# Second block of a two-block model on one core: spatial values and all heads' values projected with tokens in the partitions

## What is computed

```python
h = _rmsnorm(x, norm_w)
(q_raw, ffwd_raw, fbwd_raw, i_raw, ga_raw,
 u_raw, v_raw, gb_raw, ma_raw, mb_raw) = split(einsum('bsd,de->bse', h, w_in))     # ten pieces of 1024
y_a = _hgrn2_branch(q_raw, ffwd_raw, fbwd_raw, i_raw, ga_raw, ...)   # 8 heads of 128, values are i_raw
# the spatial branch:
u = gelu(u_raw)
v = _layernorm(gelu(v_raw), ln_w, ln_b)                              # over the 1024 channels of a token
mixed = einsum('gts,bnsgc->bntgc', w_s, v in chunks of 128 tokens and groups of 128 channels) + b_s
y_b = u * mixed * silu(g_raw)
merged = sigmoid(ma_raw) * (y_a @ w_proj_a) + sigmoid(mb_raw) * (y_b @ w_proj_b)
x = x + merged @ w_out
```

## Time and profile before

| | us |
|---|---|
| median of 3 runs (1718.98 to 1719.69) | 1719.18 |
| the profiled execution | 1719.48 |
| its span in the trace | 1717.7 |
| TensorE busy in it, matmuls | 1703.1 (99%) |
| TensorE busy in it, loads of weights | 1397.5 (81%) |
| VectorE busy | 1149.0 (67%) |
| ScalarE busy | 815.9 (48%) |
| POOL busy | 30.4 (2%) |
| granted clock of TensorE, mean | 0.999 |

### The profile page before, as it was taken

The page is one execution under the profiler, slowest core; times in us unless marked ns, Lnnn a source line. Parts: engine busy times, 40 slices in busy tenths (PEclk is TensorE's granted clock), DMA queues, the critical chain, the costliest instruction groups (busy, mean ns, idle before and its releaser), DMA issues.

```text
span 1717.7 us, 22160 instructions
## 1 busy us (share of the span) xinstructions
PE 1703.1 (99%) x8782; PEld 1397.5 (81%) x8782; DVE 1149.0 (67%) x1686; ACT 815.9 (48%) x1164; POOL 30.4 (2%) x57
## 2 busy tenths in 40 slices
PE   9999999999999999999999999999999999999997
PEld 7888888878877888888888888888888888888886
DVE  7754346878876545777775346867768778867664
ACT  6224234665756323322222334667667676665522
POOL 0000000000000000000000000100000000000000
PEclk9999999999999999999999999999999999999999
DMA  5234223333332222223223333722222222222322
GB/s 204 96 98 127 97 99 98 111 111 102 119 99 74 99 97 99 98 98 98 95 93 106 100 111 111 247 84 86 75 80 76 79 74 80 81 86 74 128 95 85
DMA packets 50551, 174.83 MB, mean 102 GB/s; under 512 B 5872, under 2 KB 8048, under 8 KB 50320
## 3 DMA queue, kind: packets, MB, share of 16 engines
q1 hardware_dynamic: 45200, 155.45, 27.4%
q0 software_dynamic: 5248, 17.96, 3.3%
HBM read 164.93 MB, written 4.26 MB: 98 GB/s over the span
## 4 chain that ended last, share of the span: by engine, by line
PE 97%; DVE 2%; ACT 1%; issue 0%; DVEq 0%; ACTq 0%
PE bank L531 85%; PE bank L785 2%; PE bank L551 2%; PE bank L713 1%; PE bank L616 1%; PE bank L795 1%; PE bank L711 1%; PE bank L671 1%; PE bank L831 0%; PE bank L820 0%; PE bank L808 0%; PE bank L692 0%; PE bank L822 0%; PE bank L824 0%; PE bank L629 0%
## 5 line engine op out<-in xcount | busy, mean ns | idle before, releaser
L531 PE MATMUL bank<-u_high,w_high 128*128 128x512 f32 x1560 | 615.4, 394 | 0.0
L531 PE MATMUL bank<-u_high,w_low 128*128 128x512 f32 x1560 | 607.8, 390 | 0.0
L531 PE MATMUL bank<-u_low,w_high 128*128 128x512 f32 x1560 | 606.9, 389 | 0.0
L896 ACT ACTIVATE w_high<-raw 128x1024 fp32r<-128x1024 f32 x283 | 298.9, 1057 | 583.5 <-PE bank L531 580.9
L1452 DVE TENSOR_TENSOR w_low<-raw,w_high 128x1024 fp32r<-128x1024 f32 x282 | 344.5, 1223 | 240.0 <-ACT w_high L896 234.4
L531 PEld LDWEIGHTS bank<-u_high,w_low 128*128 128x128 f32 x1560 | 292.8, 188 | 62.0
L531 PEld LDWEIGHTS bank<-u_high,w_high 128*128 128x128 f32 x1560 | 292.9, 188 | 61.6 <-issue 2.9
L531 PEld LDWEIGHTS bank<-u_low,w_high 128*128 128x128 f32 x1560 | 293.1, 188 | 59.9 <-issue 1.2
L1543 DVE TENSOR_TENSOR h_raw<-bank,rs 128x512 f32<-128x512 f32 x44 | 30.4, 691 | 62.2 <-PE bank L531 55.4
L531 PE MATMUL bank<-f_high,w_high 128*128 128x512 f32 x176 | 68.5, 389 | 0.0
L531 PE MATMUL bank<-f_low,w_high 128*128 128x512 f32 x176 | 68.5, 389 | 0.0
(11 more groups left out here) (362 smaller groups left out, 2432.1 us busy)
## 6 DMA issues: line engine op xcount, KB each, us to landing
raw<-stream SPq DMA_DIRECT2D x283, 512.0 KB, 3.3
rows<-running POOLq DMA_DIRECT2D x32, 256.0 KB, 3.4
X<-x_t SPq DMA_DIRECT2D x8, 256.0 KB, 5.6
u_high<-n_high_rows POOLq DMA_DIRECT2D x4, 512.0 KB, 5.0
u_low<-n_low_rows POOLq DMA_DIRECT2D x4, 512.0 KB, 5.8
residual<-X POOLq DMA_DIRECT2D x4, 512.0 KB, 8.9
X<-residual POOLq DMA_DIRECT2D x4, 512.0 KB, 5.3
masks_f<-masks SPq DMA_DIRECT2D x1, 1280.0 KB, 6.0
```

What stands on the lines that cost most here:

```text
L531: ins = pe.matmul(acc[:], w[:, k], x[:, at + k], start=start and k == first and j == 0, stop=stop and k == KT - 1 and j == 2)
L896: act.activation(w_high[:, n % HI_RING], raw[:, n % RAW_RING], ACT.Copy).then_inc(hi_done, 1)
```

## The change

The blocks `v` and `i` are replaced by four batches of 512 columns each: `("vt", 0)` and `("vt", 1)` for the spatial branch, `("it", 0)` and `("it", 1)` for the values of heads 0 to 3 and 4 to 7. A batch is four blocks of 512 KB, each with two rows of 128 input channels by 512 columns. For these the tokens stand (128x128) and the weights move: four banks of 128 tokens by 512 channels fill together, three of `ps` and one of `side`. All four batches lie in the prologue. Heads 0 to 3 then have nine blocks, heads 4 to 6 eight, head 7 nine as before; before, heads 0 and 1 had ten and the others nine.

The values land in `Ya` with tokens in the partitions, and no turn of them is left; of the mixed groups none either. GELU is applied with a scale by token (the root, turned by four matmuls of one column, `roots_by_token`) and its sum by token is kept; the squares are summed by token too, and VectorE norms with one instruction per 128 tokens (`normed`). The weight and bias of the layer norm move behind the mix: `token_sums` sums the spatial weights over tokens, `biases` makes `bs_row` of it. The second mix of each of heads 1 to 4 writes to the bank of the turns.

```diff
+BATCHES = [("vt", 0), ("vt", 1), ("it", 0), ("it", 1)]
+PER_BATCH = 4
-PROLOGUE = ([("v", j) for j in range(KT)] + [("f", 0), ("b", 0), ("q", 0), ("i", 0), ("u", 0), ("u", 1)])
+PROLOGUE = batch_blocks(*BATCHES[:3]) + [("f", 0), ("b", 0), ("q", 0)] + batch_blocks(BATCHES[3])
 FILL = [
-    [("u", 2), ("gb", 0), ("gb", 1), ("gb", 2), ("u", 3)],
-    [("gb", 3), ("u", 4), ("gb", 4), ("u", 5), ("gb", 5)],
-    [("u", 6), ("gb", 6), ("u", 7), ("gb", 7)],
-    [("mb", 0), ("mb", 1), ("mb", 2), ("mb", 3)],
+    [("u", 0), ("gb", 0), ("u", 1), ("gb", 1), ("u", 2)],
+    [("u", 3), ("gb", 2), ("u", 4), ("gb", 3), ("gb", 4)],
+    [("u", 5), ("gb", 5), ("u", 6), ("gb", 6), ("u", 7)],
+    [("gb", 7), ("mb", 0), ("mb", 1), ("mb", 2), ("mb", 3)],
     [("mb", 4), ("mb", 5), ("mb", 6), ("mb", 7)],
...
-    return [("f", h + 1), ("b", h + 1), s[0], ("i", h + 1), s[1], ("q", h + 1), ("ga", h)] + s[2:]
+    needed = [("f", h + 1), ("b", h + 1), s[0], s[1], ("q", h + 1)]
+    return needed + ([s[2], ("ga", h)] + s[3:] if len(s) > 4 else [("ga", h)] + s[2:])
...
 def half_steps(h):
     n = 2 * len(head_blocks(h))
-    if n == STEPS:
-        return [[q] for q in range(STEPS)]
-    assert n == STEPS - 2
-    return [[q] for q in range(16)] + [[16, 17], [18, 19]]
+    if n == STEPS - 2:
+        return [[q] for q in range(16)] + [[16, 17], [18, 19]]
+    assert n == STEPS - 4
+    return [[0], [1], [2], [3], [4, 5], [6, 7], [8], [9], [10, 11], [12, 13]] + [[q] for q in range(14, STEPS)]
...
-MIX_STEPS = (dict(scale=0, bias=2, turn=3, take=4, mix=5, finish=7),
-             dict(scale=9, bias=10, turn=14, take=16, mix=16, finish=18))
+MIX_STEPS = (dict(gate=2, mix=4, finish=7), dict(gate=10, mix=14, finish=18))
...
+            def batch(key, moving, ready=None):
+                b, m, n = key[:2], key[2], AT[key]
...
+                for c in range(NCH):
+                    cs = slice(c * P, (c + 1) * P)
...
+                    for a in range(2):
+                        k = 2 * m + a
...
+                        for j, (x, w) in enumerate(((xh, wh), (xl, wh), (xh, wl))):
+                            ins = pe.matmul(batch_bank(b, c)[:], x[:, k, cs], w[:, a], start=k == 0 and j == 0,
+                                            stop=k == KT - 1 and j == 2)
+                    if m == PER_BATCH - 1 and c < 3:
+                        ins.then_inc(batch_done, 1)
...
+            def roots_by_token():
+                pe.wait_ge(r_done, 1)
+                for c in range(NCH):
+                    ins = pe.matmul(side[2][:, c:c + 1], rs_b[:, c * P:(c + 1) * P], ident[:, 0:1], start=True, stop=True)
...
+            def token_sums():
+                pe.wait_ge(s_ws, 16)
+                for half in range(2):
+                    ins = pe.matmul(side[half][:], ones, ws_t[:, half * KT // 2:(half + 1) * KT // 2].rearrange("p k t -> p (k t)"),
...
+                if key == ("vt", 0, 0):
+                    stat(2, both=True)
+                if key == ("vt", 0, 2):
+                    roots_by_token()
+                if key == ("it", 0, 2):
+                    token_sums()
...
-                    wait_taken(pe, ("i", h))
-                    turn(("values", h), R[:, 2], range(NCH))
...
-                    if q == MIX_STEPS[m]["turn"]:
-                        mix_turn(j)
...
+            def evac_batch(b):
+                for c in range(NCH):
...
+                    if b[0] == "vt":
+                        ins = act.activation(columns_of(VG, b, c), src, ACT.Gelu_apprx_tanh, scale=r_tok[:, c:c + 1],
+                                             accum_out=by_token[:, 1 + b[1], c:c + 1])
+                    else:
+                        ins = act.activation(columns_of(Ya, b, c), src, ACT.Copy)
...
+                if key == ("it", 1, 2):
                     level_exp(0, 0)
+                if key == ("it", 1, 3):
                     level_exp(0, 1)
+                    evac_batch(("it", 1))
...
+                if key == ("it", 1, 0):
+                    gate_log(0)
+                if key == ("it", 1, 1):
+                    gate_sums(0, 0)
+                    gate_sums(0, 1)
+                if key == ("it", 1, 2):
+                    diff(0, 0)
+                    diff(0, 1)
+                if key == ("it", 1, 3):
                     pair(0, 0)
```

More of the change, by code:

```diff
@@ L190, in fourth_uses @@
             out += [("stat", h - 1)]
-        out += [("mix", j) for j in MIXES[h][:1]] + [("state", h, 0)]
-        out += [("state", h, 1)] + [("mix", j) for j in MIXES[h][1:]]
+        out += [("mix", j) for j in MIXES[h][:1]] + [("state", h, 0), ("state", h, 1)]
     out += [("stat", KT - 1)]
@@ L202 @@
 LATE = 2
-V_EARLY = 6
 def stream():
@@ L220, in tiles @@
 def tiles():
-    order, out = {}, {}
+    order, out, n = {}, {}, 0
     for k in STREAM:
-        out[k] = order.setdefault(k[:2], len(order))
+        if k[:2] not in order:
+            order[k[:2]] = n
+            n += 3 if k[:2] in BATCH else 1
+        out[k] = order[k[:2]]
     return out
@@ L457, in wait_taken, with batch_bank, wait_batch, wait_mixed @@
             eng.wait_ge(acc_free[TILE[key] % ACCS], TILE[key] // ACCS + 1)
+        def batch_bank(b, c):
+            return ps[(TILE[b + (0,)] + c) % ACCS] if c < 3 else side[4 - BATCH[b] % 2]
+        def wait_batch(eng, b):
+            for c in range(3):
+                n = TILE[b + (0,)] + c
+                eng.wait_ge(acc_free[n % ACCS], n // ACCS + 1)
+            eng.wait_ge(batch_taken, BATCH[b] + 1)
+        def wait_mixed(eng, j):
+            if ("mix", j) in TURN:
+                eng.wait_ge(t_done, TURN[("mix", j)] + 1)
+            else:
+                eng.wait_ge(f4_done, FOURTH[("mix", j)] + 1)
+        def mix_bank(j):
+            return side[2] if ("mix", j) in TURN else side[4]
+        def values(h, c):
+            return Ya[:, h, c * P:(c + 1) * P]
         def give(ins, key):
@@ L760, in _ @@
                            ready=None if j else (f_split, at))
-            pair_blocks(("v", 0), ("v", 1), U, s_split, KT * SECOND_EARLY,
-                        between=lambda: stat(2, both=True))
             N = (n_high_rows, n_low_rows)
[L765 to L772, removed]
+            for key in PROLOGUE:
+                if key[0] == "vt":
+                    batch(key, U, (s_split, KT * SECOND_EARLY) if key[1] == 0 else None)
+                elif key[0] == "it":
+                    if key == ("it", 1, 0):
+                        pe.wait_ge(s_moved, 16 * 8)
+                    batch(key, U if key[1] else N, None if key[1] else (s_split, KT * SECOND))
+                else:
+                    wblock(key, N)
+                if key == ("vt", 0, 0):
[4 more added lines that the diff above has]
+                    token_sums()
             def level(h, n):
@@ L819, in output @@
                     o = side[3][:, cs]
-                    pe.matmul(o, v_tok[:, c], att[:, cs], start=True, stop=False)
+                    pe.matmul(o, values(h, c), att[:, cs], start=True, stop=False)
                     if c > 0:
@@ L1399, in late @@
                     return h < KT - 1
-                return key == head_blocks(h)[7] and key in sum(VISIT[h], [])
-            before = (0, PROLOGUE[-1])
+                return key == head_blocks(h)[direct_block(h)] and key in sum(VISIT[h], [])
+            before = None
             for h in range(KT):
@@ L1409, in _ @@
                         ahead(key)
-                        if before[1][0] != "pb" and not late(*before):
+                        if before and before[1][0] != "pb" and not late(*before):
+                            if before[1][0] == "mb":
+                                wait_mixed(act, before[1][1])
                             evac(before[1], place_of(before[1]))
@@ L2089, in _ @@
                         ahead(first[q])
-                        if before[0] == "pb":
+                        if before and before[0] == "pb":
                             take_b(before)
@@ L2197, in weight_block @@
                  ssd_c=XBC + D_INNER + GROUPS * D_STATE, ssd_x=XBC, ssd_z=Z)
-    second = dict(q=Q2, f=FF2, b=FB2, i=I2, ga=GA2, u=U2, v=V2, gb=GB2, ma=MA2, mb=MB2)
+    second = dict(q=Q2, f=FF2, b=FB2, ga=GA2, u=U2, gb=GB2, ma=MA2, mb=MB2)
     whole = dict(a_out="w_a_out", o="w_o", pa="w_proj_a_2", pb="w_proj_b_2", out="w_out_2")
+    if key[:2] in BATCH:
+        at = (V2 if name == "vt" else I2) + j * T
+        return w2[2 * key[2] * P:2 * (key[2] + 1) * P, at:at + T].reshape(2, P, T).transpose(1, 0, 2)
     if name in first:
```

330 lines of the change are left out of this document (160 added, 170 removed), and 12 rows, old and new, of the table VISIT.

## The result

The changed kernel takes 1732.97 us (median of 4 runs, 1732.34 to 1733.57) against 1719.43 before (median of 4): a ratio of 1.008, 95% interval 1.0069 to 1.0092. It is slower by 13.5 us. The forecast was 1730, range 1721 to 1737.

What follows compares the result with a forecast made beforehand. TensorE bounds the kernel, with 2.6 us of slack in its heads. Terms -7.4 -1.7 -1.3 +1.7 +0.8 +0.8 +18.2 (new waits in heads 4 to 6) gave +11.1: forecast 1730 us, range 1721 to 1737.

Steps and rivals of the forecast that it cites:

- Sixteen turns: Eight turns of values and eight of mixed rows go from TensorE, 0.46 us each: 7.4 us saved.
- the two sums: Two sums over ones for the norm go from TensorE, 0.86 us each: 1.7 us saved.
- the two waits: TensorE's waits at a paired level ending the prologue (0.5 us) and at the first output (0.8) vanish: 1.3 saved.
- a late copy: End of prologue: block `f` of head 1 waits for ScalarE's copy of the values, 0.8 us, nothing to 2.5 possible.
- The waits before level 6: Heads 4 to 6, two blocks of cover gone: TensorE waits 5.6 us in heads 5 and 6, 4.2 in head 4.
- T+25.2 for pair 6: Heads 5 and 6: VectorE's pair for level 6 ends 25.2 us after T, the start of the key turns.
- The reading of the chain: ScalarE and VectorE links, each awaiting the one before, from soft gate to level 6's pair: 19.77 us before the change.
- The 1.4 us at the outputs of heads 5 and 6: VectorE needs 8.2 us from the pair to its last state, TensorE 6.8 to the output: 1.4 more wait per head.
- the dip of the clock: Sign against the forecast: a dip in the clock row of the profile after would show it wrong.
- the busy time: Sign for the forecast: TensorE's busy time in the profile after is down by about 7 us.
- 6.8 us from level 6 to the output: Heads 5 and 6: TensorE's time for level 6, a state and a block before the output, taken from the old timeline.
- The rival on the clock: Clock falls toward 1.2 GHz during the waits of heads 4 to 6, 2.5 us lost each time: 1737; chance 0.10.

Runs made afterwards that it cites:

- both: Changed kernel with steps two to a block up to step 11 and difference 5 at step 8 instead of 9: 1711.89 us, 0.9959; run again 1711.42, 0.9955.
- dead turns: Changed kernel with steps relaid, difference 5 at step 8, and 16 added turns of the identity whose results go unused: 1719.38 us.
- late merge: Changed kernel with steps in eight-block heads laid two to a block up to step 11, four to each of the last two: 1720.82 us, 1.0006.
- difference 5 early: Changed kernel with difference 5 and its exponentials at step 8 instead of 9, ahead of the gates' logarithms: 1721.53 us, 1.0011.

## Why the prediction was right, step by step

- **Turns and prologue.** Sixteen turns were put at 7.4. Heads 1 to 7 save 6.6 us with fifteen of them (by the line "both"), and the dead turns give 7.5 to 8.0 for sixteen. The trace was right to go by. The Trainium skill (TensorE: Matmul & The Clock Gate, Part 4: PE-mode transpose) has 275 ns for one transpose, an estimate of 17.6 for all of them, and the measurement decides against it as a cost of issue. Up to the output of head 0 the forecast was -0.2 (a turn, the two sums, the two waits, `token_sums`, `roots_by_token`, a late copy); measured -0.18. `roots_by_token` takes 0.95 in the trace (0.8 forecast), `token_sums` 1.88 (1.7), the late copy costs 0.6 (0.8).
- **The waits before level 6.** Forecast T+25.2 for pair 6 and T+19.6 for TensorE, 5.6 us. Level 6 started at T+25.2, 5.6 late, of which the rows show 5.37 as waits (2.07 and 3.30). The soft gate started at T+5.85 (6.0 in the forecast), and pair 6 ended 19.2 behind it (19.24). In head 4 4.2 was forecast, 3.8 came (0.47 and 3.30). The reading of the chain link by link held, and so did the claim that only two missing blocks count: the block moved to head 4 took the loss away there.
- **What was off.** The 1.4 us at the outputs of heads 5 and 6 did not show. Two of my cases came together, forecast and clock: in each of the three heads the clock fell to 1.2 GHz around level 6, and in heads 5 and 6 TensorE was so much slower behind it (2.2 and 2.4 us) that VectorE was ready. Two of the signs that the prediction gave came out against it, the dip of the clock and the busy time, which did not fall by 7. The mis-sized term is "6.8 us from level 6 to the output": it was 9.2 (1555.95 to 1565.12). Instead of 7.0 the ledger has 7.8 and 8.0 for heads 5 and 6 (with the turn added back), and 5.7 instead of 4.2 for head 4. Together 21.4 for 18.2, which is the 3 us between 1730 and 1733. The sum also lacked the 0.8 us less behind the last matmul and the 0.2 of the first block, which no term forecast and which made it look a little better than it was.
- **The rival on the clock** was priced 2.5 a head on top of the waits. The size of a fall is right in heads 5 and 6 (2.2 and 2.4) and too high in head 4 (1.6), but it was added to a wait at the output that it in truth replaces, so it cost 1 us net in heads 5 and 6. I gave it too little weight with a chance of 0.10, on the ground of one gap at the end of the kernel before. The Trainium skill (TensorE: Matmul & The Clock Gate, HAM oscillation) has idle gaps bring the half clock back; the three falls here agree with it, while two of the three gaps of 1.8 us in the late merge brought none.
- **A question that the prediction did not ask** is whether the chain had to be that long. Difference 5 behind the logarithms stood in the prediction's own chain as a link; nothing but the order of steps made it one.

## What to carry to other kernels

When a change takes work off the bounding engine, count what that work was covering, place by place: 7 us were saved everywhere and 21 lost where two blocks of cover went from between a start and a deadline of the other engines' chain. Before giving such a change up, look at how the steps lie over the blocks that are left, and at links of the chain that are there by order and not by data; two edits of a table turned 1.008 into 0.996. If an engine is full in the stretch, moving its work within it only moves the wait; start the stretch sooner.

## What the runs showed that I had not expected

A single wait is not enough to say whether the clock falls. The late merge has the same gap of 1.8 us between levels 5 and 6 in heads 4, 5 and 6 (1.73, 1.78, 1.78), yet only head 5 shows a fall. Three windows, one over each of them:

```profile
1434.00:1441.00 7.00, 5.27 (x57) 4.38 (x57) 6.86 (x11) 6.88 (x11) 0.00 (x0) 1.00 0.21 77
1490.00:1500.00 10.00, 8.22 (x59) 6.52 (x58) 9.65 (x17) 8.13 (x11) 0.00 (x0) 0.83 0.16 52
1547.00:1557.00 10.00, 8.20 (x66) 6.38 (x64) 9.65 (x17) 5.50 (x8) 0.00 (x0) 1.00 0.14 52
```

It cost head 5 about 1.5 us over head 6 (13.39 and 11.93). In the kernel with difference 5 early it was head 6 alone that fell. Both kernels scatter more (1719.07 to 1722.22 and 1720.79 to 1723.01 over ten runs each) than the one with dead turns, which has no such wait (1719.23 to 1719.81, ten runs). The mean granted clock is on record for every run. In the late merge it goes with the span: five runs at 0.998 have spans of 1717.2 to 1718.1, five at 0.996 or 0.997 have 1719.1 to 1719.7. With difference 5 early the two overlap (1718.8 to 1719.5 at 0.998, 1718.8 to 1720.2 below). So falls that come and go are the likely reason, above all for the late merge; in which heads they fell is known only for the one run of each that has its trace.
